# A two-layer hybrid decoder step: gated product and sum of the branches in PSUM, the residual rebuilt by pairs behind the mix, one gate chunk rounded ahead of a wait

## The chip, the cores and the metric

The kernel runs on one core of a Trainium2 chip. The metric is the time of one execution on the device, in microseconds; the median of three runs of the kernel before is 1038.56 us (1033.41 to 1039.5).

## What is computed

One inference step of a decoder with two layers, for 256 prompt tokens and 32 sample tokens (288 columns), model width 1024. Cut to what matters here:

```python
z = x @ w_in                                   # conv branch, attention branch, g_a, g_b
conv_out = silu(layer_norm(conv)) @ w_conv_out
attn_out = o @ w_attn_out                      # o: three gated attentions
mixed = sigmoid(g_a) * conv_out + sigmoid(g_b) * attn_out
x = layer_norm(ALPHA * x + mixed @ w_o, ln1_g, ln1_b)
h = silu(x @ w_gate) * (x @ w_up)
x = layer_norm(ALPHA * x + h @ w_down, ln2_g, ln2_b)
```

All is fp32. Activations are kept transposed: 128 channels on the partitions, 288 tokens in the free dimension, so `x` is 8 blocks of 128x288, and `h` is 22.

## The kernel before

**Products in three parts.** To multiply in fp32 with the `fp32r` format, each operand is split in a rounded high part and the rest, its low part. Each 128x128 block of weights costs three matmuls: high by high (L692, L730, L713), low weight by high (L693, L731, L714) and high weight by low (L694, L732, L715).

**Weights.** They come in 116 chunks per layer, of 8 blocks of 128x128 (512 KB). Each chunk goes through a ring: SyncE loads it into one of three raw buffers (`wch`), as soon as GpSimd is done with the chunk three before; ScalarE writes its high part (`high_part`, L1103, `w_hi<-wch`), as soon as TensorE is done with the chunk three before; GpSimd writes the low part (`low_part`, L620, four instructions of 128x256, `w_lo<-wch,w_hi`); TensorE then uses it. Each engine works through its program in the order in which it is written, and all waits are on semaphores written out by hand; there is no scheduler. So where a `high_part` stands among ScalarE's other instructions decides when GpSimd gets its work.

**Outputs.** Each output block of 128x288 goes to one of two PSUM banks (`proj`), in turn. TensorE starts an output when the one two before has been read (`out_read`) and its weights' low part is there (`lo_ready`).

**The stage around the change.** Per layer:

- Branch outputs: 8 blocks of `conv_out`, then 8 of `attn_out` (`branch_out`, 12 matmuls each, two blocks to a chunk). The gates stand as tanh in `gate_a` and `gate_b` (both inside the tile `hid`, which is the name in the profile). For each block VectorE runs `merge` (L1850): gate = (gate + 1) * bank. That is sigmoid times the branch, times 2.
- The mix: after each of the 8 `attn_out` blocks VectorE adds both products (L1929, `hid<-hid`), ScalarE rounds the sum to `mix_hi` (L1108), VectorE writes `mix_lo` (L1926, `low_mixed`). After every second block ScalarE also does one `high_part`.
- Ahead of the mix VectorE rebuilds the residual `x` from its high and low part in one instruction over 2304 columns (L1921, `res<-x_hi,x_lo`, signal `x_sum`), and ScalarE multiplies it by ALPHA, also in one (L1108, `res<-res`, signal `ax_ready`).
- Output projection `w_o`: 8 blocks of 24 matmuls, here WO0 to WO7. VectorE adds each to the residual (L1598, `features_in`), and from the fifth on the statistics of the layer norm are worked out.
- Feed-forward: gate and up blocks in turn, 24 matmuls each, here GU0 to GU43. For each pair ScalarE applies tanh, then rounds two chunks (`high_part`), the first of which in a layer waits behind the first normalised gate block (`gate_normed`, L1966).

The second layer runs the same program.

Of the kernel before, what the change touches and what calls it, by code (L numbers as in the profile page):

```python
# [19 lines left out]
F32 = mybir.dt.float32  # L20
F32R = mybir.dt.float32r
I32 = mybir.dt.int32
ALU = mybir.AluOpType
ACT = mybir.ActivationFunctionType
# [4 lines left out]
TOK = SEQ + DEC_B * DEC_T  # L29
# [117 lines left out]
def decoder_kernel(nc, xT, consts, page_table, weights, small, w1, w2, cmp_pages, slc_pages, win, past_u,  # L147
                   yT, kv_out, p_conv_out, s_conv_out, win_out):
    with ExitStack() as ctx:
# [124 lines left out]
        conv_mean, conv_var = ps_g[:, 0:TOK], ps_m[:, 0:TOK]  # L274
        seed_ps, mean_ps, square_ps = ps_o[:, 0:TOK], ps_s[:, 0, 0:TOK], ps_s[:, 1, 0:TOK]
        sum_ps = ps_w[:, 0:TOK]
        second_squares, third_squares = ps_t[:, :, 0:TOK], ps_s[:, :, 0:TOK]
        rstd_ps, tanh_ps, up_ps, product_ps = ps_w[:, 0:TOK], ps_o[:, 0:TOK], ps_g[:, 0:TOK], ps_s[:, 1, 0:TOK]
        SEED = KD // 2
# [72 lines left out]
        gpt_act = Signal("gpt_act", 2)  # L352
        uexp = Signal("uexp", 8)
        upt_ready = Signal("upt_ready", 8)
        ax_ready = Signal("ax_ready", 1)
        x_ready = Signal("x_ready", 2 * KD)
        ffn_tanh = Signal("ffn_tanh", KF)

# [12 lines left out]
        normed = Signal("normed", 10)  # L371
        nsa_ready = Signal("nsa_ready", 1)
        x_lo_ready = Signal("x_lo_ready", 3 * KD)
        x_sum = Signal("x_sum", 1)
        hid_lo_ready = Signal("hid_lo_ready", KF)
        gate_normed = Signal("gate_normed", KF)
        hid_ready = Signal("hid_ready", KF)
# [706 lines left out]
        def _(act):  # L1084
# [11 lines left out]
            def high_part(layer, n):  # L1096

                user, back = before(n, CHUNKS, PAIRS)
                act.wait_ge(*chunk_in[n % SLOTS](layer, n // SLOTS + 1))

                signal, count = last_use(user)
                act.wait_ge(*signal(layer, count - back * signal.per_layer))
                hi_ready.up(nc.scalar.activation(w_hi[:, n % PAIRS].rearrange("p k n -> p (k n)"),  # L1103
                                                 wch[:, n % SLOTS].rearrange("p k n -> p (k n)"), ACT.Copy))

            def do(out, in_, func, sig=None, wait=True, **kw):

                i = nc.scalar.activation(out, in_, func, **kw)  # L1108
                sig = sig or act_order
                n = sig.up(i)  # L1110
                if wait:
                    act.wait_ge(*sig(now["layer"], n))
# [154 lines left out]
            with layers(act) as layer:  # L1267
# [133 lines left out]

                for which in range(2):
                    if which == 0:
                        act.wait_ge(*x_sum(layer, 1))
                        do(res[:], res[:], ACT.Copy, ax_ready, scale=ALPHA)
                        for c in range(KD):
                            act.wait_ge(*mixed_ready(layer, c + 1))
                            do(mix_hi[:, c], gate_a[:, c], ACT.Copy, x_hi_ready, wait=False)
                            if c % 2:
                                high_part(layer, CH_IN + (KD + c) // 2 + PAIRS)  # L1410
                        for n in range(KD - 1):
                            high_part(layer, CH_IN + CH_MIX + PAIRS + n)
                            if n == 1:
                                do(warm[:], eps[:, 0:1], ACT.Sqrt, wait=False)
                            if n == SEED:
                                for pair in range(2):
                                    features_square(layer, 0, pair)
                                    features_high(layer, 2 * pair)
                                    features_high(layer, 2 * pair + 1)
                            if n >= SEED:  # L1420
                                features_square(layer, 0, n - 2)
                                features_high(layer, n)
                        features_square(layer, 0, KD - 3)
                        features_high(layer, KD - 1)
                        features_root(layer, 0)
                        high_part(layer, CH_IN + CH_MIX + PAIRS + KD - 1)
                        do(warm[:], eps[:, 0:1], ACT.Tanh, wait=False)
                    else:
                        for i in range(KF):
                            act.wait_ge(*gate_normed(layer, i + 1))  # L1430
                            do(gate_n, normed_g, ACT.Identity, bias=sums_of[:, i % 2, 1:2])
                            if i:
                                act.wait_ge(*hid_ready(layer, i))
                            do(tanh_ps, gate_n, ACT.Tanh, ffn_tanh, wait=False, scale=0.5)
                            high_part(layer, FIRST_GU + 2 * i + PAIRS)
                            high_part(layer, FIRST_GU + 2 * i + PAIRS + 1)
                            if 2 <= i < 2 + KD:
                                c = i - 2
                                act.wait_ge(*normed(layer, 3 + c // 2))
                                do(resv[:, c], resv[:, c], ACT.Identity, x_ready, scale=alpha_gb[:, c:c + 1],  # L1440
                                   bias=alpha_gb[:, KD + c:KD + c + 1], wait=False)
                            act.wait_ge(*hid_ready(layer, i + 1))
                            do(hid_hi[:, i], product_ps, ACT.Copy, hid_hi_ready, wait=False)
                        do(warm[:], eps[:, 0:1], ACT.Sqrt, wait=False)
                        n = SEED
                        for c in range(CH_DOWN - 1):
                            if n < KD - 1 and 8 * c + 7 >= KF * (n + 1) + 8:
                                if n == SEED:
                                    features_square(layer, 1, 0)
                                    features_square(layer, 1, 1)  # L1450
                                features_square(layer, 1, n - 2)
                                n += 1
                            j = CHUNKS - CH_DOWN + PAIRS + c
                            high_part(*((layer, j) if j < CHUNKS else (layer + 1, j - CHUNKS)))
                        assert n == KD - 1
                        features_square(layer, 1, n - 2)
                        features_root(layer, 1)
                        high_part(layer + 1, 2)
                        gn, bn = s("g2"), s("b2")
                        for c in range(KD):  # L1460
                            if c % 2 == 0:
                                act.wait_ge(*normed(layer, 7 + c // 2))
                            do(resv[:, c], resv[:, c], ACT.Identity, x_ready, scale=gn[:, c:c + 1], bias=bn[:, c:c + 1], wait=False)
                            if c:
                                act.wait_ge(*x_ready(layer, KD + c))
                                do(x_hi[:, c - 1, 0:TOK], resv[:, c - 1], ACT.Copy, x_hi_ready, wait=False)
                        act.wait_ge(*x_ready(layer, 2 * KD))
                        do(x_hi[:, KD - 1, 0:TOK], resv[:, KD - 1], ACT.Copy, x_hi_ready, wait=True)
                        do(warm[:], eps[:, 0:1], ACT.Tanh, wait=False)
# [7 lines left out]
        def _(dve):  # L1477
# [15 lines left out]
            def do(i, sig=None, wait=True):  # L1493
                sig = sig or dve_order
                n = sig.up(i)
                if wait:
                    dve.wait_ge(*sig(now["layer"], n))
# [85 lines left out]
            def features_in(layer, which, low):  # L1583
# [10 lines left out]

                for n in range(KD):
                    o = first + n
                    dve.wait_ge(*out_done(layer, o + 1))
                    read_out(o, v.scalar_tensor_tensor(out=resv[:, n], in0=bank[o % 2][:, 0:TOK], scalar=0.5, in1=resv[:, n],  # L1598
                                                       op0=ALU.mult, op1=ALU.add))
# [165 lines left out]
            with layers(dve) as layer:  # L1765
# [152 lines left out]
                low_attention(1, slice(3, 4))  # L1918

                dve.wait_ge(*ut_done(layer, 8))  # L1920
                do(v.tensor_tensor(resv, x_hi[:, :, 0:TOK].bitcast(F32), x_lo[:, :, 0:TOK].bitcast(F32), ALU.add), x_sum)  # L1921

                def low_mixed(c):

                    dve.wait_ge(*x_hi_ready(layer, c + 1))
                    do(v.tensor_tensor(mix_lo[:, c], gate_a[:, c], mix_hi[:, c].bitcast(F32), ALU.subtract), x_lo_ready, wait=False)  # L1926
                for n in range(KD):
                    merge(KD + n)
                    do(v.tensor_tensor(gate_a[:, n], gate_a[:, n], gate_b[:, n], ALU.add), mixed_ready, wait=False)  # L1929
                    if n:  # L1930
                        low_mixed(n - 1)
                low_mixed(KD - 1)

                def low_shifted(c):

# [18 lines left out]
                    read_out(o, v.scalar_tensor_tensor(out=out, in0=mean_sb, scalar=sums_at[:, 0:1], in1=bank[o % 2][:, 0:TOK],  # L1954
                                                       op0=ALU.mult, op1=ALU.add))

                dve.wait_ge(*ax_ready(layer, 1))
                features_in(layer, 0, low_shifted)
                take_variance(layer, 0, sd)
                for i in range(KF):  # L1960
# [123 lines left out]
```

## Time and profile before

| | |
|---|---|
| median of three runs | 1038.56 us (1033.41, 1038.56, 1039.5) |
| the profiled execution | 1034.15 us |
| its span, first to last instruction | 1032.4 us |
| mean granted clock of TensorE | 0.989 |
| TensorE matmuls busy | 979.1 us, 95% |
| GpSimd busy | 753.1 us, 73% |
| VectorE busy | 602.1 us, 58% |
| ScalarE busy | 524.2 us, 51% |

All rows below are of the profiled execution; times count from the start of its span, and 1.75 us lie around it. PE is TensorE, PEld its weight loads, DVE VectorE, ACT ScalarE, POOL GpSimd, SPq SyncE's DMA queue. In a row of the timeline the first number is the start, the second the length (of all its instructions, if x2 and more), and in brackets stands how long the engine had been idle before it and what ended that.

### The profile page before, as it was taken

Reading aid. Unit: us, or ns where it says so; the run is one execution under the profiler, and the core shown is the slowest. Engines: PE = TensorE matmul, PEld = TensorE weight load, DVE = VectorE, ACT = ScalarE, POOL = GpSimd, SP = SyncE. Lnnn points to the kernel's source line nnn. Section 1 sums busy time; section 2 is a strip of 40 time slices with the busy share of each in tenths; the row PEclk is TensorE's granted clock in tenths of the full one; section 3 lists DMA queues with packets and bytes.
Section 4 is the critical chain, followed back from the end, with each engine's and each line's share of the span. In section 5 each row is a group of like instructions: output and inputs, shape, how many; then the busy total and the mean of one; then the engine's idle time right before and its main releaser. Section 6 shows DMA issues by size and latency. Waiting matters only on the chain.

```text
span 1032.4 us, 23314 instructions
## 1 busy us (share of the span) xinstructions
PE 979.1 (95%) x7438; PEld 929.8 (90%) x7438; DVE 602.1 (58%) x1370; ACT 524.2 (51%) x966; POOL 753.1 (73%) x1081
## 2 busy tenths in 40 slices
PE   6999989999999999999999999899999999999996
PEld 6997878788989999999999978887789999999996
DVE  2969675567577555512457895844775765554125
ACT  4352674455556655533454335654545565555335
POOL 7877745434978888898867785634369788889985
PEclk9999999999999999999999999999999999999998
DMA  8985686612546755555457566684225354555543
GB/s 287 308 276 188 194 274 213 231 63 63 168 153 205 246 189 164 163 180 159 138 175 235 170 184 203 225 263 167 63 82 164 126 165 163 164 165 176 168 144 108
DMA packets 78917, 185.09 MB, mean 179 GB/s; under 512 B 9538, under 2 KB 42690, under 8 KB 78530
## 3 DMA queue, kind: packets, MB, share of 16 engines
q1 hardware_dynamic: 70288, 167.03, 50.0%
q10 hardware_dynamic: 8354, 15.59, 4.6%
q8 instruction: 62, 1.02, 0.5%
q0 software_dynamic: 144, 0.89, 0.3%
q14 instruction: 69, 0.57, 0.2%
HBM read 170.90 MB, written 12.57 MB: 178 GB/s over the span
## 4 chain that ended last, share of the span: by engine, by line
POOL 52%; issue 25%; PE 20%; POOLq 1%; DMA 1%; DVE 1%; ACT 1%; ACTq 0%; SPq 0%; DVEq 0%
POOL w_lo L620 46%; PE proj L692 4%; PE proj L694 4%; PE proj L693 4%; POOL hid L644 3%; POOL res L642 3%; PE proj L715 2%; PE proj L713 2%; PE proj L714 2%; DMA res<-xT_in 1%; POOLq L639 0%; POOLq L614 0%; POOL res L651 0%; DVE res L1575 0%; DVE sig_u L1642 0%
## 5 line engine op out<-in xcount | busy, mean ns | idle before, releaser
L620 POOL TENSOR_TENSOR w_lo<-wch,w_hi 128x256 fp32r<-128x256 f32 x940 | 685.9, 765 | 262.1 <-ACT w_hi L1103 261.8
L692 PE MATMUL proj<-x_hi,w_hi 128*128 128x290 f32 (+1 forms) x1248 | 381.9, 306 | 16.6 <-POOL w_lo L620 13.5
L694 PE MATMUL proj<-x_lo,w_hi 128*128 128x290 f32 (+1 forms) x1248 | 373.5, 299 | 0.0
L693 PE MATMUL proj<-x_hi,w_lo 128*128 128x290 f32 (+1 forms) x1248 | 372.6, 299 | 0.0
L1103 ACT ACTIVATE w_hi<-wch 128x1024 fp32r<-128x1024 f32 x235 | 247.7, 1055 | 145.2 <-PE proj L715 84.2
L692 PEld LDWEIGHTS proj<-x_hi,w_hi 128*128 128x128 f32 x1248 | 238.7, 191 | 22.2 <-DVE x_lo L1489 9.6
L693 PEld LDWEIGHTS proj<-x_hi,w_lo 128*128 128x128 f32 x1248 | 239.1, 192 | 0.6
L694 PEld LDWEIGHTS proj<-x_lo,w_hi 128*128 128x128 f32 x1248 | 238.5, 191 | 0.0
L713 PE MATMUL proj<-hid_hi,w_hi 128*128 128x288 f32 x352 | 104.4, 296 | 0.0
L715 PE MATMUL proj<-hid_lo,w_hi 128*128 128x288 f32 x352 | 104.1, 296 | 0.0
L714 PE MATMUL proj<-hid_hi,w_lo 128*128 128x288 f32 x352 | 103.5, 294 | 0.0
L1514 DVE SCALAR_TENSOR_TENSOR ps_s<-u_p,sm,ps_s 128x256 f32<-128x256 f32 x232 | 94.5, 483 | 4.2
L1598 DVE SCALAR_TENSOR_TENSOR res<-proj,res 128x288 f32<-128x288 f32 x32 | 14.6, 455 | 132.8 <-PE proj L715 111.2
L1953 DVE COPY sums_of<-proj 128x2 f32<-128x2 f32 x88 | 14.0, 159 | 99.7 <-PE proj L694 99.5
L714 PEld LDWEIGHTS proj<-hid_hi,w_lo 128*128 128x128 f32 x352 | 66.3, 188 | 0.1
L713 PEld LDWEIGHTS proj<-hid_hi,w_hi 128*128 128x128 f32 x352 | 66.1, 188 | 0.1
L715 PEld LDWEIGHTS proj<-hid_lo,w_hi 128*128 128x128 f32 x352 | 66.0, 187 | 0.0
L1108 ACT ACTIVATE q_raw<-q_raw,sums_of 128x288 f32<-128x288 f32 x44 | 23.6, 537 | 75.4 <-DVE q_raw L1966 75.4
L1108 ACT ACTIVATE res<-res,unit_top 128x128 f32<-128x128 f32 (+2 forms) x96 | 37.6, 394 | 31.8 <-DVE unit_top L1671 31.7
L692 PE MATMUL proj<-mix_hi,w_hi 128*128 128x288 f32 x128 | 38.9, 304 | 0.6 <-POOL w_lo L620 0.6
L693 PE MATMUL proj<-mix_hi,w_lo 128*128 128x288 f32 x128 | 37.8, 295 | 0.0
L694 PE MATMUL proj<-mix_lo,w_hi 128*128 128x288 f32 x128 | 37.7, 294 | 0.0
(288 smaller groups left out, 1519.7 us busy)
## 6 DMA issues: line engine op xcount, KB each, us to landing
wch<-weights_in SPq DMA_DIRECT2D x235, 512.0 KB, 3.7
pg<-slc_pages_in SPq DMA_DIRECT2D x128, 128.0 KB, 2.5
pg<-cmp_pages_in SPq DMA_DIRECT2D x96, 128.0 KB, 3.1
wn<-win_in SPq DMA_DIRECT2D x16, 512.0 KB, 5.1
win_out<-wn ACTq DMA_DIRECT2D x4, 2048.0 KB, 9.5
pg<-cmp_pages_in ACTq DMA_DIRECT2D x32, 128.0 KB, 4.5
hid<-w_in SPq DMA_DIRECT2D x2, 1024.0 KB, 6.1
kv_out<-kv ACTq DMA_DIRECT2D x2, 864.0 KB, 3.5
```

What stands on the lines that cost most here:

```text
L620: last = nc.gpsimd.tensor_tensor(lo[:, cols], raw[:, cols], hi[:, cols].bitcast(F32), ALU.subtract)
L642: do(nc.gpsimd.tensor_tensor(dst, u_s[:, :, :, tap:tap + DEC_T], tap_weight(conv_w[:, :, tap]), ALU.mult))
L644: do(nc.gpsimd.tensor_tensor(out, out, tap_s[:], ALU.add))
L692: mm(ps, hi[:, kb], x[0][:, kb, 0:n], start=kb == 0, stop=False)
L693: mm(ps, lo[:, kb], x[0][:, kb, 0:n], start=False, stop=False)
L694: last = mm(ps, hi[:, kb], x[1][:, kb, 0:n], start=False, stop=kb == KD - 1)
L713: mm(ps, hi, hid_hi[:, kb], start=kb == 0, stop=False)
L714: mm(ps, lo, hid_hi[:, kb], start=False, stop=False)
L715: last = mm(ps, hi, hid_lo[:, kb], start=False, stop=kb == KF - 1)
L1103: hi_ready.up(nc.scalar.activation(w_hi[:, n % PAIRS].rearrange("p k n -> p (k n)"), wch[:, n % SLOTS].rearrange("p k n -> p (k n)"), ACT. ...
L1108: i = nc.scalar.activation(out, in_, func, **kw)
L1514: i = v.scalar_tensor_tensor(out=out, in0=in_, scalar=conv_w[:, c, tap:tap + 1], in1=so_far, op0=ALU.mult, op1=ALU.add)
```

## The change

1. `merge` of the `attn_out` blocks no longer writes back over the gate in SBUF: the product goes to a PSUM bank (`sum_ps`, in the tile `ps_w`), and the sum with the `conv_out` product to one of four other PSUM places (`mixed_ps`, in `ps_s` and `ps_t`), in turn. ScalarE and `low_mixed` read it there.
2. The rebuild of `x` is cut in four instructions of two blocks (576 columns), and stands behind the last `low_mixed`, no longer ahead of the first merge. ScalarE's scaling by ALPHA is cut alike and stands behind the eight `mix_hi`, between the `high_part`s of `w_o`'s chunks. `features_in` waits for the pairs one by one.
3. In the feed-forward the `high_part` of chunk GU3 moves ahead of the wait for the first normalised gate block.

```diff
+        mixed_ps = [ps_s[:, 0, 0:TOK], ps_s[:, 1, 0:TOK], ps_t[:, 0, 0:TOK], ps_t[:, 1, 0:TOK]]
...
-        ax_ready = Signal("ax_ready", 1)
+        ax_ready = Signal("ax_ready", 4)
...
-        x_sum = Signal("x_sum", 1)
+        x_sum = Signal("x_sum", 4)
...
                     if which == 0:
-                        act.wait_ge(*x_sum(layer, 1))
-                        do(res[:], res[:], ACT.Copy, ax_ready, scale=ALPHA)
+                        def scale_x(n):
+                            act.wait_ge(*x_sum(layer, n + 1))
+                            do(resv[:, 2 * n:2 * n + 2], resv[:, 2 * n:2 * n + 2], ACT.Copy, ax_ready, wait=False, scale=ALPHA)
                         for c in range(KD):
                             act.wait_ge(*mixed_ready(layer, c + 1))
-                            do(mix_hi[:, c], gate_a[:, c], ACT.Copy, x_hi_ready, wait=False)
+                            do(mix_hi[:, c], mixed_ps[c % 4], ACT.Copy, x_hi_ready, wait=False)
                             if c % 2:
                                 high_part(layer, CH_IN + (KD + c) // 2 + PAIRS)
+                        scale_x(0)
                         for n in range(KD - 1):
+                            if n < 3:
+                                scale_x(n + 1)
                             high_part(layer, CH_IN + CH_MIX + PAIRS + n)
...
                     else:
+                        high_part(layer, FIRST_GU + PAIRS)
                         for i in range(KF):
                             act.wait_ge(*gate_normed(layer, i + 1))
...
-                            high_part(layer, FIRST_GU + 2 * i + PAIRS)
+                            if i:
+                                high_part(layer, FIRST_GU + 2 * i + PAIRS)
                             high_part(layer, FIRST_GU + 2 * i + PAIRS + 1)
...
                 for n in range(KD):
                     o = first + n
+                    if which == 0 and n in (0, 2, SEED):
+                        dve.wait_ge(*ax_ready(layer, n // 2 + (2 if n == SEED else 1)))
                     dve.wait_ge(*out_done(layer, o + 1))
...
                 dve.wait_ge(*ut_done(layer, 8))
-                do(v.tensor_tensor(resv, x_hi[:, :, 0:TOK].bitcast(F32), x_lo[:, :, 0:TOK].bitcast(F32), ALU.add), x_sum)
+
+                def add_x(n):
+                    blocks = slice(2 * n, 2 * n + 2)
+                    do(v.tensor_tensor(resv[:, blocks], x_hi[:, blocks, 0:TOK].bitcast(F32), x_lo[:, blocks, 0:TOK].bitcast(F32), ALU.add),
+                       x_sum, wait=False)
 
                 def low_mixed(c):
 
                     dve.wait_ge(*x_hi_ready(layer, c + 1))
-                    do(v.tensor_tensor(mix_lo[:, c], gate_a[:, c], mix_hi[:, c].bitcast(F32), ALU.subtract), x_lo_ready, wait=False)
+                    do(v.tensor_tensor(mix_lo[:, c], mixed_ps[c % 4], mix_hi[:, c].bitcast(F32), ALU.subtract), x_lo_ready, wait=False)
                 for n in range(KD):
-                    merge(KD + n)
-                    do(v.tensor_tensor(gate_a[:, n], gate_a[:, n], gate_b[:, n], ALU.add), mixed_ready, wait=False)
+                    o = O_MIX + KD + n
+                    if n:
+                        dve.wait_ge(*mixed_ready(layer, n))
+                    dve.wait_ge(*out_done(layer, o + 1))
+                    read_out(o, v.scalar_tensor_tensor(out=sum_ps, in0=gate_b[:, n], scalar=1.0, in1=bank[o % 2][:, 0:TOK],
+                                                       op0=ALU.add, op1=ALU.mult))
+                    do(v.tensor_tensor(mixed_ps[n % 4], gate_a[:, n], sum_ps, ALU.add), mixed_ready, wait=False)
                     if n:
                         low_mixed(n - 1)
                 low_mixed(KD - 1)
+                for n in range(4):
+                    add_x(n)
...
-                dve.wait_ge(*ax_ready(layer, 1))
                 features_in(layer, 0, low_shifted)
```

VectorE, from the low part of the attention output into the mix, before:

```order
L1859 TENSOR_TENSOR attn_lo<-u_p,attn_hi 128x288
L1921 TENSOR_TENSOR res<-x_hi,x_lo 128x2304
L1849 REGISTER_ALU
L1850 SCALAR_TENSOR_TENSOR hid<-hid,proj 128x288
L1502 REGISTER_ALU
L1929 TENSOR_TENSOR hid<-hid 128x288
```

and now:

```order
L1868 TENSOR_TENSOR attn_lo<-u_p,attn_hi 128x288
L1944 REGISTER_ALU
L1945 SCALAR_TENSOR_TENSOR ps_w<-hid,proj 128x288
L1509 REGISTER_ALU
L1947 TENSOR_TENSOR ps_s<-hid,ps_w 128x288
```

The 2304-column rebuild is gone from between them, and the product and the sum have PSUM tiles as their outputs.

VectorE, from the last two low parts of the mix to the reading of WO0, now (before, L1598 followed L1926 at once):

```order
L1939 TENSOR_TENSOR mix_lo<-ps_t,mix_hi 128x288
L1933 TENSOR_TENSOR res<-x_hi,x_lo 128x576 x4
L1605 ISA
L1606 REGISTER_ALU
L1607 SCALAR_TENSOR_TENSOR res<-proj,res 128x288
```

The four pieces of the rebuild stand between the mix and the first read of a bank of `w_o`.

ScalarE, from the last two `mix_hi` to the fifth chunk of `w_o` and beyond, now (before, the scalings were one instruction `res<-res` of 128x2304 ahead of the first `mix_hi`):

```order
L1109 ACTIVATE mix_hi<-ps_t 128x288 x2
L1100 REGISTER_ALU
L1103 REGISTER_ALU
L1104 ACTIVATE w_hi<-wch 128x1024
L1406 ISA
L1109 ACTIVATE res<-res 128x576
L1406 REGISTER_ALU
L1109 ACTIVATE res<-res 128x576
L1100 REGISTER_ALU
L1103 REGISTER_ALU
L1104 ACTIVATE w_hi<-wch 128x1024
```

Two scalings stand ahead of the `high_part` of WO3, one ahead of that of WO4 and one ahead of that of WO5.

ScalarE at the start of the feed-forward, before:

```order
L1103 ACTIVATE w_hi<-wch 128x1024
L1108 ACT_TABLE_LOAD
L1108 ACTIVATE warm<-eps 128x1
L1430 ISA
L1108 ACTIVATE q_raw<-q_raw,sums_of 128x288
L1112 REGISTER_ALU
L1108 ACTIVATE ps_o<-q_raw 128x288
```

and now:

```order
L1104 ACTIVATE w_hi<-wch 128x1024
L1109 ACT_TABLE_LOAD
L1109 ACTIVATE warm<-eps 128x1
L1100 REGISTER_ALU
L1103 REGISTER_ALU
L1104 ACTIVATE w_hi<-wch 128x1024
L1436 ISA
L1109 ACTIVATE q_raw<-q_raw,sums_of 128x288
```

The high part of GU3 stands ahead of the wait and of the first gate block's bias; that of GU4 follows the tanh alone.

## Rows read from the trace of the kernel before

**Rows 1.** Page, part 1: busy time and share of each engine.

```profile
PE 979.1 (95%) x7438; PEld 929.8 (90%) x7438; DVE 602.1 (58%) x1370; ACT 524.2 (51%) x966; POOL 753.1 (73%) x1081
```

**Rows 2.** Waits of PE: line, waited for, us in total, times, longest.

```profile
PE proj L692 <- POOL w_lo L620: 14.1, 7, 9.6
...
PE proj L730 <- DVE hid L1850: 2.8, 2, 1.4
...
PE proj L730 <- POOL w_lo L620: 0.8, 2, 0.4
```

**Rows 3.** Timeline of PE, first layer, from the mix to GU3.

```profile
249.82 0.29 PE L732 MATMUL proj<-attn_lo,w_hi 128*128 128x288 f32 x1
251.52 0.39 PE L730 MATMUL proj<-attn_hi,w_hi 128*128 128x288 f32 x1 [1.41 <-DVE hid L1850]
251.75 0.30 PE L731 MATMUL proj<-attn_hi,w_lo 128*128 128x288 f32 x1
...
258.56 0.40 PE L730 MATMUL proj<-attn_hi,w_hi 128*128 128x288 f32 x1 [0.42 <-POOL w_lo L620]
262.29 0.40 PE L692 MATMUL proj<-mix_hi,w_hi 128*128 128x288 f32 x1 [0.29 <-POOL w_lo L620]
303.16 0.40 PE L692 MATMUL proj<-x_hi,w_hi 128*128 128x290 f32 x1 [1.50 <-POOL w_lo L620]
```

**Rows 4.** Timeline of DVE, first layer, rebuild, mix and a sum in PSUM.

```profile
247.84 2.98 DVE L1921 TENSOR_TENSOR res<-x_hi,x_lo 128x2304 f32<-128x2304 f32 x1
...
256.00 0.99 DVE L1926 TENSOR_TENSOR mix_lo<-hid,mix_hi 128x288 fp32r<-128x288 f32 x1
256.92 0.44 DVE L1850 SCALAR_TENSOR_TENSOR hid<-hid,proj 128x288 f32<-128x288 f32 x1
257.40 0.52 DVE L1929 TENSOR_TENSOR hid<-hid 128x288 f32<-128x288 f32 x1
...
258.74 0.44 DVE L1850 SCALAR_TENSOR_TENSOR hid<-hid,proj 128x288 f32<-128x288 f32 x1
...
273.05 0.47 DVE L1603 TENSOR_TENSOR ps_w<-ps_w,res 128x288 f32<-128x288 f32 x1
```

**Rows 5.** Timeline of ACT, first layer, scaling, first and second `high_part` of the mix.

```profile
250.85 2.13 ACT L1108 ACTIVATE res<-res 128x2304 f32<-128x2304 f32 x1 [3.84 <-DVE res L1921]
253.69 1.05 ACT L1103 ACTIVATE w_hi<-wch 128x1024 fp32r<-128x1024 f32 x1
```

**Rows 6.** POOL, groups by form: 255 to 265.5 us, then 272 to 279 us.

```profile
L620 POOL TENSOR_TENSOR w_lo<-wch,w_hi 128x256 fp32r<-128x256 f32 x12 | 11.0, 951 | 6.4 <-ACT w_hi L1103 6.4
...
L620 POOL TENSOR_TENSOR w_lo<-wch,w_hi 128x256 fp32r<-128x256 f32 x11 | 7.7, 744 | 0.0
```

**Rows 7.** DVE and POOL, end of the first layer: 576 columns with two inputs in SBUF.

```profile
512.75 1.17 DVE L1575 TENSOR_TENSOR res<-res,sig_u 128x576 f32<-128x576 f32 x1
514.62 1.19 DVE L1575 TENSOR_TENSOR res<-res,sig_u 128x576 f32<-128x576 f32 x1
517.54 0.75 DVE L1575 TENSOR_TENSOR res<-res,sig_u 128x576 f32<-128x576 f32 x1
...
513.26 4.04 POOL L620 TENSOR_TENSOR w_lo<-wch,w_hi 128x256 fp32r<-128x256 f32 x4
```

**Rows 8.** ACT, then POOL, at the start of the feed-forward of the first layer.

```profile
296.53 0.20 ACT L1108 ACTIVATE warm<-eps 128x1 f32<-128x1 f32 x1
298.26 0.54 ACT L1108 ACTIVATE q_raw<-q_raw,sums_of 128x288 f32<-128x288 f32 x1 [1.53 <-DVE q_raw L1966]
299.19 1.99 ACT L1103 ACTIVATE w_hi<-wch 128x1024 fp32r<-128x1024 f32 x2
...
295.30 2.82 POOL L620 TENSOR_TENSOR w_lo<-wch,w_hi 128x256 fp32r<-128x256 f32 x4 [3.45 <-ACT w_hi L1103]
300.31 11.16 POOL L620 TENSOR_TENSOR w_lo<-wch,w_hi 128x256 fp32r<-128x256 f32 x16 [2.19 <-ACT w_hi L1103]
```

**Rows 9.** Engines' busy time from GU3 to near the feed-forward's end.

```profile
303.20:500.00 196.80, 196.80 (x1466) 196.69 (x1467) 93.72 (x214) 98.70 (x138) 173.49 (x247) 1.00 0.57 184
```

## The prediction

> **What bounds the kernel now.** I read the page's busy times first: TensorE's matmuls are busy 95% of the span, no other engine over 73% [rows 1]. The change touches no matmul, so it can only take away time in which TensorE waits. Other engines' own idle time costs nothing by itself. So the next view is what TensorE waited for [rows 2]: 14.1 us on GpSimd's low parts, 2.8 us on VectorE's merge ahead of a branch output, twice, and 0.8 us there on GpSimd, twice. Of the 14.1 us, 9.6 are one wait at the start, which the change doesn't touch.
>
> The third view is TensorE's timeline from the mix to GU3 [rows 3]. The reader is to see four holes: 1.41 us before block 10 of the branch outputs (251.52), 0.42 us before block 14 (258.56), 0.29 us before WO0 (262.29) and 1.50 us before GU3 (303.16). A hole costs more than its idle time, as matmuls overlap: from 249.82 to 251.52 is 1.70 us where 0.13 is usual (in the feed-forward 1466 matmuls fill 196.8 us [rows 9]), and the next follows after 0.23, so 1.57 + 0.10 = 1.67 us are lost, the idle time and 0.26 more. By the same surcharge the others cost 0.68, 0.55 and 1.76. Together 4.66 us a layer; the second layer has the same (the counts of 2 in [rows 2]). That is 9.3 us, the most that the change can give, but for hesitations too small for these rows.
>
> **Why the holes are there.** VectorE starts the 2304-column rebuild at 247.84 and is in it for 2.98 us [rows 4]; the merge of block 8, which frees the bank for block 10, stands behind it. ScalarE waits 3.84 us for the rebuild, scales for 2.13 us, and so gets to its next `high_part` at 253.69 only [rows 5]. GpSimd, which had been idle 6.4 us, then works without a break but slowly: 951 ns for an instruction that takes 744 later [rows 6]. That is where VectorE's L1929 and L1926 run, both with two inputs in SBUF, and L1926 itself takes 0.99 us [rows 4]. So blocks 14 and 15 and WO0 wait for late low parts.
>
> **Part 1, the rebuild out of the way.** Block 9's twelve matmuls end with the one at 249.82 [rows 3], so block 8 ends at about 248.4, and VectorE is free since 247.8: the merge is done by 248.9, and block 10 starts on time, at 249.95 (249.82 + 0.13). The first hole goes: 1.67. ScalarE can round the second sum when block 9 is merged and added (out at 250.1, two instructions of 0.48, so 251.1), and starts the `high_part` at 251.5 in place of 253.69. GpSimd starts at 252.7.
>
> **Part 2, product and sum in PSUM.** Each of the three VectorE instructions of a block then has at most one input in SBUF. Price of the PSUM form: L1603 (one PSUM input, PSUM output) takes 0.47, the merge with its PSUM input 0.44 to 0.45 [rows 4]; no row has the merge with a PSUM output. I take 0.46 for each, bounded by 0.44 from below and, from above, by the 0.52 of L1929 among GpSimd's work. GpSimd's four instructions then take 4 x 0.695 = 2.8 us a chunk (7.7 us for 11 is 0.70 each [rows 6]), not 3.65. Block 14's chunk is ready at 255.5, needed at 249.95 + 4 x 1.58 = 256.3; WO0's is ready at 258.6, needed at 259.4; WO1's at 261.7, needed at 262.6. The second and third hole go: 0.68 + 0.55. VectorE's cadence changes from 1.82 us a block (256.92 to 258.74 [rows 4]) to about 1.35, under TensorE's 1.58 (12 matmuls at 0.132).
>
> **Part 3, what the rebuild costs where it now stands.** It isn't hidden there. `low_mixed` of block 7 ends at about 261.5, and the four pieces of 576 columns follow, when GpSimd is at work (WO2's low part, from 262.1). The nearest rows are L1575, also 576 columns with two SBUF inputs: 0.75 us by itself, 1.17 and 1.19 beside GpSimd, whose four instructions then take 4.04 us [rows 7]. That is 1.24 over 2.8: two pieces at 0.52 and one 288-column instruction at 0.21 (951 less 744 [rows 6]). So both alternate, at 0.6 + 0.69 = 1.3 us a piece: the pieces start at about 261.6, 262.9, 264.1 and 265.4, and three of them fall among WO2's four: 262.1 + 2.8 + 3 x 0.52 and some waiting for a first piece = 266.7. TensorE wants WO2 at 259.4 + 2 x 3.17 = 265.8. The read of WO0's bank, queued behind the pieces, ends at 266.5, and WO2 needs that too. Either way a new hole: idle 0.9, and with the surcharge 1.2 us. Bounds: nothing, if the pieces don't meet GpSimd (0.75 each, done by 264.5); 2.2 us if each piece meets a whole instruction of it. I take 1.2, since rows 7 show just this pair.
>
> The Trainium skill (SBUF — State Buffer, Who interferes with whom) says that a VectorE instruction with two SBUF inputs and a GpSimd instruction that reads SBUF exclude each other for the whole instruction, and one with at most one SBUF input doesn't contend. The trace agrees that they exclude each other, but shows a GpSimd instruction delayed by 0.52 us beside 0.75 of VectorE's. By the rule's whole instruction the new hole would be some 0.7 us a layer larger (3 x 0.23), and the forecast 1.4 us later.
>
> ScalarE's scalings: one of 2.13 us before [rows 5], four of about 0.65 now, 0.5 us more in sum, between the high parts of WO3 to WO5. TensorE needs WO3 at 270.0, and GpSimd, done with WO2 at 266.7, has it by 269.5, ScalarE's high part being there at 265.3. WO4's slack is 0.9 us and WO5's 1.2, though its load waits for the late WO2. Cost 0; if that cover went, 0.5 us.
>
> **Part 4, GU3 ahead of the wait.** ScalarE is done with its table and the warm-up at 296.73 and sits idle 1.53 us for the first gate block [rows 8]. GU0, whose buffer GU3 takes, is long out. The `high_part` fits in: 296.8 to 297.8, and the gate at 298.26 isn't delayed. GpSimd, free at 298.12, starts GU3 then and not at 300.31 [rows 8]: done at 300.9, needed at 301.4. The fourth hole goes: 1.76. What is late next is GU5, whose high part still hangs on the gate block of the next pair, GU2, which doesn't move: it comes about when TensorE wants it, so a few tenths may come back here; I take 0. In the 196.8 us from GU3 on the matmuls have no hole at all [rows 9], so the ring can hold that pace, narrowly.
>
> **Sum.** A layer: 1.67 + 0.68 + 0.55 - 1.2 + 1.76 = 3.46 us, two layers 6.9 us. Against the profiled execution's 1034.15 us (span 1032.4 and 1.75 around it) that is 1027.2. The runs shown lie in two places, 1033.41 beside the profiled 1034.15, and 1038.56 and 1039.5; the median is in the upper, and gives 1031.6. I predict in between, 1029.5 us. A measurement of this kernel tells about 1% (10.4 us) from no change, and 6.9 is 0.7%.
>
> **Rivals.**
> - *The rebuild stays hidden.* If the pieces slip through between chunks, for VectorE gets its turn sooner than in rows 7, the whole 9.3 us come: 1024.9 by the profiled execution, 1029.3 by the median. For it: GpSimd pauses 0.4 us (261.7 to 262.1) just when the first piece starts. Against: rows 7.
> - *A hole only moves.* TensorE ahead by some 3 us finds the next link late: GU5, which comes just in time at best, or loads whose order on SyncE's queue stays tied to GpSimd. With 1 us back at GU5 and 1 us in WO3 to WO5, each layer, 2.9 us are left: 1031.2 to 1035.6. For it: slacks under 1.3 us all along part 3. Against: rows 9; in the feed-forward the links hang on TensorE's own pace.
> - *PSUM operands make VectorE the bound (slower).* Three instructions a block, all with PSUM on a side. At 0.25 us more each the cadence is 2.1 us a block, against TensorE's 1.58: the mix then ends 7 x 0.5 = 3.6 us late, and with the 1.2 for the rebuild that eats all 4.66. Slower from there on: at 0.35 us more it is 2.4, 8 x 0.3 = 2.4 us a layer further, 1039 to 1043. Against: 0.47 for L1603 and 0.44 for the merge.
>
> **Chances.** The forecast 0.50, the hidden rebuild 0.22, the moved hole 0.22, the slower case 0.06. The range: down to 1023 (the hidden rebuild, less 2 for small hesitations that go too), up to 1036 (the moved hole from the median). Faster by over 1%: half of the hidden rebuild, which lands at 0.9%, and a quarter of the forecast, as the executions scatter by 5 us: 0.24. Slower by over 1% only at the slower case's end: 0.03. Within 1%: 0.73.
>
> **What would show it.** Right: no idle time before block 10, block 14, WO0 and GU3; L620 at about 745 ns through the mix; merges 1.58 us apart; a hole of about 0.9 us before WO2, with L620 over 1200 ns three times beside the 576-column pieces. Wrong: `low_mixed` or the sum above 0.55 us; no hole before WO2 (then the first rival); holes before WO3 to WO5 or GU5, on GpSimd (the second); a granted clock off 0.989, which would change more than all of this.

## The result and the profile after

The changed kernel takes 1029.08 us (median of 8 runs, 1027.48 to 1030.35). The kernel before, run beside it and counted with its earlier three, takes 1035.47 us (8 runs, 1033.41 to 1039.5). The ratio is 0.9931, 95% interval 0.9911 to 0.9952: 6.4 us less, against a forecast of 6.9 and a predicted time of 1029.5. The profiled executions have spans of 1032.4 and 1025.7 us, 6.7 apart, with granted clocks of 0.989 and 0.991.

What TensorE waited for, after (line, waited for, us in total, times, longest), the answer to [rows 2]:

```profile
PE proj L693 <- POOL w_lo L621: 11.9, 5, 9.7
...
PE proj L731 <- DVE attn_lo L1868: 0.7, 2, 0.3
```

The wait for the merge (2.8 us) and the one of L730 for GpSimd (0.8 us) are gone from the list. Of the 11.9 us, 9.7 are the wait at the start. The timeline of PE shows in the mix, `w_o` and the feed-forward of each layer one hole only, where [rows 3] have four:

```profile
266.75 0.29 PE L694 MATMUL proj<-mix_hi,w_lo 128*128 128x288 f32 x1
266.89 0.29 PE L695 MATMUL proj<-mix_lo,w_hi 128*128 128x288 f32 x1
267.81 0.40 PE L693 MATMUL proj<-mix_hi,w_hi 128*128 128x288 f32 x1 [0.64 <-POOL w_lo L621]
268.05 0.30 PE L694 MATMUL proj<-mix_hi,w_lo 128*128 128x288 f32 x1
...
772.41 0.40 PE L693 MATMUL proj<-mix_hi,w_hi 128*128 128x288 f32 x1 [0.65 <-POOL w_lo L621]
```

That is the first matmul of WO2. From 266.89 to 267.81 are 0.92 us, 0.13 are usual, and the next follows after 0.24, so 0.79 + 0.11 = 0.90 us are lost.

VectorE, after, the answer to [rows 4]:

```profile
248.25 0.70 DVE L1868 TENSOR_TENSOR attn_lo<-u_p,attn_hi 128x288 fp32r<-128x288 f32 x1 [0.58 <-ACT attn_hi L1109]
249.71 0.46 DVE L1945 SCALAR_TENSOR_TENSOR ps_w<-hid,proj 128x288 f32<-128x288 f32 x1 [0.76 <-PE proj L733]
250.20 0.46 DVE L1947 TENSOR_TENSOR ps_s<-hid,ps_w 128x288 f32<-128x288 f32 x1
251.30 0.46 DVE L1945 SCALAR_TENSOR_TENSOR ps_w<-hid,proj 128x288 f32<-128x288 f32 x1 [0.64 <-PE proj L733]
...
257.65 0.46 DVE L1945 SCALAR_TENSOR_TENSOR ps_w<-hid,proj 128x288 f32<-128x288 f32 x1 [0.27 <-PE proj L733]
258.15 0.46 DVE L1947 TENSOR_TENSOR ps_s<-hid,ps_w 128x288 f32<-128x288 f32 x1
258.52 0.45 DVE L1939 TENSOR_TENSOR mix_lo<-ps_s,mix_hi 128x288 fp32r<-128x288 f32 x1
259.23 0.46 DVE L1945 SCALAR_TENSOR_TENSOR ps_w<-hid,proj 128x288 f32<-128x288 f32 x1 [0.27 <-PE proj L733]
...
262.63 4.54 DVE L1933 TENSOR_TENSOR res<-x_hi,x_lo 128x576 f32<-128x576 f32 x4
267.10 1.02 DVE L1607 SCALAR_TENSOR_TENSOR res<-proj,res 128x288 f32<-128x288 f32 x2
```

The low part takes 0.45 us where it took 0.99. A block takes 1.58 us (257.65 to 259.23), and VectorE now waits 0.27 us in each for TensorE. The four pieces take 4.54 us; where nothing holds them up the same columns take 2.74 (the run with one input in SBUF, below), so 1.8 are waiting.

GpSimd, groups, after: the mix (253.5 to 263 us), then WO2's chunk (263 to 267.8 us), the answer to [rows 6]:

```profile
L621 POOL TENSOR_TENSOR w_lo<-wch,w_hi 128x256 fp32r<-128x256 f32 x12 | 8.5, 743 | 4.9 <-ACT w_hi L1104 4.9
...
L621 POOL TENSOR_TENSOR w_lo<-wch,w_hi 128x256 fp32r<-128x256 f32 x5 | 5.2, 1071 | 0.3 <-ACT w_hi L1104 0.3
```

951 ns became 743 in the mix, and 1071 beside the rebuild. The last of WO2's four instructions, and VectorE's read of WO0's bank, which frees it for WO2:

```profile
266.52 1.24 POOL L621 TENSOR_TENSOR w_lo<-wch,w_hi 128x256 fp32r<-128x256 f32 x1
267.10 0.44 DVE L1607 SCALAR_TENSOR_TENSOR res<-proj,res 128x288 f32<-128x288 f32 x1
```

GpSimd ends at 267.76, the read at 267.54, and the matmul starts at 267.81. So GpSimd is the last link, but the read is only 0.2 us ahead of it (in the second layer too: 772.36 and 772.13, for 772.41).

The start of the feed-forward, ACT and then POOL, the answer to [rows 8]:

```profile
295.28 0.20 ACT L1109 ACTIVATE warm<-eps 128x1 f32<-128x1 f32 x1
295.39 1.04 ACT L1104 ACTIVATE w_hi<-wch 128x1024 fp32r<-128x1024 f32 x1
297.02 0.54 ACT L1109 ACTIVATE q_raw<-q_raw,sums_of 128x288 f32<-128x288 f32 x1 [0.59 <-DVE q_raw L1985]
...
294.05 8.43 POOL L621 TENSOR_TENSOR w_lo<-wch,w_hi 128x256 fp32r<-128x256 f32 x12 [3.44 <-ACT w_hi L1104]
```

The high part of GU3 fills 1.04 us of what was idle time, the gate block behind it still waits 0.59 us for VectorE, and GpSimd goes from GU2 to GU3 and GU4 without a break.

**A ruler for the stage.** The executions differ by several us in places that have nothing to do with the change. So I measure the stretch from the matmul of block 8 that waits 0.33 us for the attention's low part to the first matmul of `w_down`. It holds all that was changed. Before and after, first layer:

```profile
247.86 0.40 PE L730 MATMUL proj<-attn_hi,w_hi 128*128 128x288 f32 x1 [0.33 <-DVE attn_lo L1859]
...
435.58 0.29 PE L713 MATMUL proj<-hid_hi,w_hi 128*128 128x288 f32 x1
```

```profile
249.00 0.40 PE L731 MATMUL proj<-attn_hi,w_hi 128*128 128x288 f32 x1 [0.33 <-DVE attn_lo L1868]
...
432.60 0.29 PE L714 MATMUL proj<-hid_hi,w_hi 128*128 128x288 f32 x1
```

| kernel | stretch, layer 1 and 2 (us) | less than before, both layers |
|---|---|---|
| before | 187.72, 187.66 | |
| after | 183.60, 183.66 | 8.12 |

8.12 us are gained there, and some 1.4 given back elsewhere: in the first layer the stretch starts 1.14 us later (249.00 against 247.86), between the stretches 0.33 more pass, behind them as much as before. The programs are the same up to that start, and it lies anywhere from 247.60 to 251.03 us in the runs below, among kernels with the same code ahead of it. So I count this as scatter of the executions. In part it is the clock: it is granted at 1.00 through both stretches in all ten traces, and falls to 0.50, the lower of its two levels (1.2 of 2.4 GHz), twice ahead of the first. In the kernel that starts latest (251.03) it is at 0.50 from 173.5 to 180.0 us, where the changed kernel has 1.00 again from 178.4 on; TensorE has a long wait for ScalarE just there: 3.2 us up to 174.6 us, and 2.7 up to 173.6 in the changed kernel. What the rest of the scatter comes of was not tried.

### The profile page after: what moved, and what is told of

The parts are those of the page before. It is cut to its first block, busy times and chain, and to the rows that moved or that the text cites. A ratio compares the mean times of both kernels' runs of the same rounds, so it can differ in the third digit from the quotient of the medians.

```text
span 1025.7 us, 23332 instructions
## 1 busy us (share of the span) xinstructions
PE 976.8 (95%) x7438; PEld 928.7 (91%) x7438; DVE 601.6 (59%) x1376; ACT 524.8 (51%) x972; POOL 753.3 (73%) x1081
## 4 chain that ended last, share of the span: by engine, by line
POOL 53%; issue 24%; PE 20%; POOLq 1%; DMA 1%; DVE 1%; ACT 1%; ACTq 0%; SPq 0%; DVEq 0%
POOL w_lo L621 46%; PE proj L693 4%; PE proj L695 4%; PE proj L694 4%; POOL hid L645 3%; POOL res L643 3%; PE proj L716 2%; PE proj L715 2%; PE proj L714 2%; DMA res<-xT_in 1%; POOLq L640 0%; POOLq L615 0%; POOL res L652 0%; DVE res L1582 0%; DVE sig_u L1651 0%
## 6 DMA issues: line engine op xcount, KB each, us to landing
hid<-w_in SPq DMA_DIRECT2D x2, 1024.0 KB, 6.0
```

## The experiments

The ratios are to the kernel before, run beside them: 1035.82 us (median of 31 runs) for the first four, 1035.42 us (11 runs) for the last four. "Lost" is counted from start to start of the matmuls, as above. A hesitation is a matmul that starts up to 0.1 us late, too little for its row to show idle time.

### The high part of GU3 alone

The kernel before, with this:

```diff
                     else:
+                        high_part(layer, FIRST_GU + PAIRS)
                         for i in range(KF):
...
-                            high_part(layer, FIRST_GU + 2 * i + PAIRS)
+                            if i:
+                                high_part(layer, FIRST_GU + 2 * i + PAIRS)
```

> The kernel before with part 4 alone (the high part of GU3 ahead of the wait). My theory: the four holes are independent, so the hole before GU3 (1.50 us idle, 1.76 lost) goes in both layers and the three others stay: from the low part of the attention output to GU3's first matmul 53.5 us in place of 55.3, span 3.5 us shorter, no new hole at GU5. Rival (a hole only moves): half of it or more comes back as idle time before GU5 or a later gate block, and the span is under 2 us shorter.

Measured: 1032.33 us (10 runs), ratio 0.9963 (0.9949 to 0.9977). The stretch takes 186.00 and 185.89 us: 1.72 and 1.77 less. The profiled span, 1033.6 us, is longer than before's, but its stretch starts only at 251.03. PE's holes:

```profile
254.69 0.39 PE L730 MATMUL proj<-attn_hi,w_hi 128*128 128x288 f32 x1 [1.41 <-DVE hid L1852]
261.73 0.40 PE L730 MATMUL proj<-attn_hi,w_hi 128*128 128x288 f32 x1 [0.42 <-POOL w_lo L620]
265.46 0.39 PE L692 MATMUL proj<-mix_hi,w_hi 128*128 128x288 f32 x1 [0.31 <-POOL w_lo L620]
```

The three holes of the mix stand as they were, the fourth is gone, and nothing new comes at GU5 or later. The rival is out, and the 1.76 us are a term by themselves.

### The change without the high part of GU3

The changed kernel with the last edit undone.

> The changed kernel without part 4. My theory: the hole before GU3 is back with 1.50 us idle, the rest is as in the changed kernel: that stretch takes 52.9 us (51.1 in the changed kernel), the span is 3.5 us longer than the changed kernel's. Rival (TensorE being earlier, the high part of GU3 comes later relative to it): over 2 us idle there.

Measured: 1032.24 us (10 runs), ratio 0.9962 (0.9947 to 0.9977); the stretch 185.40 and 185.38 us, 1.80 and 1.72 more than the changed kernel's.

```profile
267.71 0.40 PE L693 MATMUL proj<-mix_hi,w_hi 128*128 128x288 f32 x1 [0.64 <-POOL w_lo L621]
301.81 0.40 PE L693 MATMUL proj<-x_hi,w_hi 128*128 128x290 f32 x1 [1.51 <-POOL w_lo L621]
```

The hole before GU3 is back with the idle time it had. It doesn't depend on what happens in the mix. The spans were 2.5 us apart (1028.2 and 1025.7) where I expected 3.5. The missing 1.0 lies between the two stretches, where 320.02 us pass here and 320.99 in the changed kernel, in code that is the same.

### Product and sum in PSUM alone

The kernel before, with the rebuild in one piece ahead of the mix, but:

```diff
-                            do(mix_hi[:, c], gate_a[:, c], ACT.Copy, x_hi_ready, wait=False)
+                            do(mix_hi[:, c], mixed_ps[c % 4], ACT.Copy, x_hi_ready, wait=False)
...
-                    do(v.tensor_tensor(mix_lo[:, c], gate_a[:, c], mix_hi[:, c].bitcast(F32), ALU.subtract), x_lo_ready, wait=False)
+                    do(v.tensor_tensor(mix_lo[:, c], mixed_ps[c % 4], mix_hi[:, c].bitcast(F32), ALU.subtract), x_lo_ready, wait=False)
...
-                    merge(KD + n)
-                    do(v.tensor_tensor(gate_a[:, n], gate_a[:, n], gate_b[:, n], ALU.add), mixed_ready, wait=False)
...
+                    read_out(o, v.scalar_tensor_tensor(out=sum_ps, in0=gate_b[:, n], scalar=1.0, in1=bank[o % 2][:, 0:TOK],
+                                                       op0=ALU.add, op1=ALU.mult))
+                    do(v.tensor_tensor(mixed_ps[n % 4], gate_a[:, n], sum_ps, ALU.add), mixed_ready, wait=False)
```

> The kernel before with part 2 alone: product and sum in PSUM, the rebuild in one piece ahead of the mix. My theory: the hole before block 10 stays at 1.41 us idle, since the rebuild makes it; GpSimd's instructions in the mix fall from 951 to about 745 ns, so its chunk for block 14 is ready at about 0.2 us before it is wanted and the holes before block 14 and WO0 go with the two hesitations: 1.6 us a layer, span 3 us shorter. Rival (those holes come of ScalarE's late high part, 253.69, not of the port): they stay, within 0.3 us.

Measured: 1032.95 us (10 runs), ratio 0.9973 (0.9957 to 0.9988); the stretch 186.09 and 186.12 us, 1.63 and 1.54 less than before. POOL in the mix (255 to 267 us), and PE's one hole there:

```profile
L621 POOL TENSOR_TENSOR w_lo<-wch,w_hi 128x256 fp32r<-128x256 f32 x15 | 10.6, 745 | 6.9 <-ACT w_hi L1104 6.9
```

```profile
252.96 0.40 PE L731 MATMUL proj<-attn_hi,w_hi 128*128 128x288 f32 x1 [1.42 <-DVE ps_w L1933]
302.98 0.40 PE L693 MATMUL proj<-x_hi,w_hi 128*128 128x290 f32 x1 [1.50 <-POOL w_lo L621]
```

GpSimd starts as late as before, after 6.4 us of idle time, and yet the holes before block 14 and WO0 are gone. So the late start alone doesn't make them; it takes the instructions with two inputs in SBUF, beside which GpSimd needs 951 ns in place of 745 ("the port" in what follows). The rival, that they stay, is out. For block 14 the late start counts as well: with the move alone (next) GpSimd starts 2.2 us earlier, counted from the stretch's start, and is as slow as before, and that hole is gone too. It needed both. The hole before block 10 doesn't depend on where product and sum go.

### The move alone

The kernel before, with rebuild and scaling cut and moved behind the mix as in the change; product and sum in SBUF.

```diff
-                do(v.tensor_tensor(resv, x_hi[:, :, 0:TOK].bitcast(F32), x_lo[:, :, 0:TOK].bitcast(F32), ALU.add), x_sum)
...
                 low_mixed(KD - 1)
+                for n in range(4):
+                    add_x(n)
```

> The kernel before with the rebuild and the scaling cut and moved behind the mix, product and sum still in SBUF, GU3 not moved. My theory: block 10's hole goes (1.67 us), but GpSimd still takes 3.65 us a chunk in the mix where TensorE takes 3.17, so it falls behind by 0.5 us a chunk, and the pieces cost it 1.6 us more at WO2: idle before WO0, WO1 and WO2 of together 2 to 3 us a layer, so that the move alone gives between -0.5 and +1 us a layer and the span changes by less than 2 us. Rival (the move is what gives the gain): 2.5 us a layer, span 5 us shorter.

Measured: 1036.02 us (10 runs), ratio 0.9999 (0.998 to 1.0018); the stretch 187.83 and 187.85 us, 0.11 and 0.19 more than before.

```profile
259.70 0.40 PE L693 MATMUL proj<-mix_hi,w_hi 128*128 128x288 f32 x1 [0.29 <-POOL w_lo L621]
262.68 0.40 PE L693 MATMUL proj<-mix_hi,w_hi 128*128 128x288 f32 x1 [0.33 <-DVE mix_lo L1937]
263.60 0.40 PE L693 MATMUL proj<-mix_hi,w_hi 128*128 128x288 f32 x1 [0.26 <-DVE mix_lo L1937]
268.88 0.39 PE L693 MATMUL proj<-mix_hi,w_hi 128*128 128x288 f32 x1 [1.42 <-DVE res L1605]
```

The holes before blocks 10 and 14 are gone, and as much comes back: the four here lose 0.55, 0.59, 0.52 and 1.68 us with the matmuls behind them, 3.34 in all, where the mix lost 3.30 before. Two of them I hadn't named: VectorE itself is late with `mix_lo`, at 1.82 us a block. The last is released by the read of WO0's bank behind the pieces, 1.0 us after GpSimd's low part (268.76 against 267.77). The move gains nothing while VectorE and GpSimd stand in each other's way in the mix.

### The rebuild with one input in SBUF

The changed kernel, but the pieces add what stands in a PSUM place to `x_hi`; the residual is then not `x_hi` + `x_lo`, and all that follows is computed from that.

```diff
-                    do(v.tensor_tensor(resv[:, blocks], x_hi[:, blocks, 0:TOK].bitcast(F32), x_lo[:, blocks, 0:TOK].bitcast(F32), ALU.add),
+                    do(v.tensor_tensor(resv[:, blocks], x_hi[:, blocks, 0:TOK].bitcast(F32), ps_t[:, :, 0:TOK], ALU.add),
```

> The changed kernel, but the four pieces of the rebuild take their second input from a PSUM place (what stands there in the tile ps_t) and not from x_lo in SBUF; so the residual is not the sum of high and low part. Same place, same number, same columns. My theory (the new hole before WO2 is the port that VectorE and GpSimd share): the pieces take 0.70 to 0.75 us each and are through 2.9 us after the first starts (4.54 in the changed kernel), L621 stays at 745 ns for WO2's low part in place of 1250, the hole before WO2 (0.64 us idle, 0.90 lost) is gone in both layers, the stretch from the attention's low part to the first matmul of w_down takes 182.7 us in place of 183.6. Rival (the hole is the bank of WO0, read behind the pieces, or ScalarE's scalings): the hole stays at over 0.4 us.

Measured: 1026.0 us (4 runs), ratio 0.9909 (0.9891 to 0.9927); the stretch 182.68 and 182.62 us, and PE has no hole before WO2. DVE's timeline and POOL's group from 262.9 to 267.5 us:

```profile
262.38 2.74 DVE L1933 TENSOR_TENSOR res<-x_hi,ps_t 128x576 f32<-128x576 f32 x4
265.03 0.45 DVE L1607 SCALAR_TENSOR_TENSOR res<-proj,res 128x288 f32<-128x288 f32 x1
...
L621 POOL TENSOR_TENSOR w_lo<-wch,w_hi 128x256 fp32r<-128x256 f32 x7 | 4.9, 739 | 0.3 <-ACT w_hi L1104 0.3
```

Same place, same columns, same number: 2.74 us in place of 4.54, and GpSimd at 739 ns. The hole is the port's; ScalarE's scalings, which stand where they stood, cost nothing. (This kernel can't tell GpSimd's delay from that of the bank read behind the pieces, since both go with the port. The ends in the changed kernel's trace, above, put GpSimd's last, by 0.2 us.)

### Some pieces early, the rest behind

The changed kernel with three pieces back in the mix, where GpSimd is idle:

```diff
                 for n in range(KD):
                     o = O_MIX + KD + n
+                    if n < 3:
+                        add_x(n)
...
-                for n in range(4):
-                    add_x(n)
+                add_x(3)
```

> The changed kernel with three pieces of the rebuild back in the mix, one ahead of each of the first three merges, where GpSimd is idle (249.7 to 253.7 us), and the fourth behind the mix. My theory: each delays VectorE by 0.7 us, of which the idle time there (0.76, 0.64, 0.27 us) takes most, the low parts of block 14 and WO0 come 0.5 us later than in the changed kernel but still just in time, and the hole before WO2 goes: the stretch takes 182.7 us, span 1.8 us shorter than the changed kernel's. Rival (slack too small): holes before block 14 and WO0 of 0.2 us or more each take the place of the one at WO2.

Measured: 1026.04 us (6 runs), ratio to before 0.9916 (0.9897 to 0.9936); span 1024.0 us; the stretch 182.74 and 182.72 us, 0.86 and 0.94 less than the changed kernel's, and no hole before block 14, WO0 or WO2. The pieces:

```profile
248.73 1.17 DVE L1933 TENSOR_TENSOR res<-x_hi,x_lo 128x576 f32<-128x576 f32 x1
250.68 0.75 DVE L1933 TENSOR_TENSOR res<-x_hi,x_lo 128x576 f32<-128x576 f32 x1
252.58 0.75 DVE L1933 TENSOR_TENSOR res<-x_hi,x_lo 128x576 f32<-128x576 f32 x1
262.38 0.89 DVE L1933 TENSOR_TENSOR res<-x_hi,x_lo 128x576 f32<-128x576 f32 x1
```

The first still meets the end of a GpSimd instruction (1.17), the next two meet none (0.75). The same with two early and two behind:

> As the last, with two pieces early and two behind the mix. My theory: the first late piece starts before GpSimd has WO2's high part, the second costs it 0.5 us: WO2's low part is done some 0.2 us before TensorE wants it. No hole, or one under 0.1 us; the stretch takes 182.7 to 182.9 us. Rival: hole before WO2 of 0.3 us or more.

Measured: 1026.9 us (6 runs), ratio 0.9915 (0.9898 to 0.9931), the stretch 182.78 and 182.72 us, no hole. And with all four early:

> As e6, with all four pieces early, one ahead of each of the first four merges. My theory: the fourth meets GpSimd at block 14's chunk (0.5 us) and delays the fourth merge by over 1 us, so WO0's chunk is late: holes before block 14 or WO0 of together 0.3 to 1.4 us idle, and the stretch is 183 to 184.3 us. Rival: VectorE has caught up, no hole, 182.7 us.

Measured: 1027.06 us (4 runs), ratio 0.9914 (0.9896 to 0.9932), the stretch 182.99 us in both layers. Here I was wrong: no idle time over 0.1 us appears before block 14 or WO0, only two hesitations, so 0.25 us are lost and not 0.3 to 1.4. The stretch lies at the lower end of what I gave. The fourth piece cost GpSimd's chunk 0.6 us, near the 0.5 that I had (3.45 us for four instructions, where 2.84 is usual), but the fourth merge came 0.93 us late and not over 1, and VectorE had caught up three blocks later:

```profile
255.42 0.75 DVE L1933 TENSOR_TENSOR res<-x_hi,x_lo 128x576 f32<-128x576 f32 x1
256.09 0.46 DVE L1947 SCALAR_TENSOR_TENSOR ps_w<-hid,proj 128x288 f32<-128x288 f32 x1
...
260.11 0.46 DVE L1947 SCALAR_TENSOR_TENSOR ps_w<-hid,proj 128x288 f32<-128x288 f32 x1 [0.26 <-PE proj L733]
```

(In the changed kernel the fourth merge starts 5.47 us after the stretch's first matmul, here 6.40; the idle time before the seventh, the last row, is back to 0.26.)

The ruler tells these three kernels from the changed one (1.80, 1.76 and 1.28 us less over both layers); the ratios, whose intervals overlap with the changed kernel's, don't. Of those that compute everything, three early and one behind has the shortest profiled span, 1024.0 us, and the lowest median, 1026.04, but two early and two behind is 0.04 us away by the ruler, which is nothing.

## Why the prediction was right, and what was off

- **What bounds it.** TensorE's holes were all that could be gained, and they were gained: the four are gone.
- **The four terms.** GU3: 1.76 forecast, 1.72 and 1.77 by itself. Block 14 and WO0 together: 1.23 forecast; the PSUM edit alone gives 1.63 and 1.54, because two hesitations of about 0.2 us each (with the matmul behind) went with them, at mix_lo's last block in WO0 and at WO1, which I had left out of the sum. Block 10: 1.67, gone by the move. The first hesitation, in the kernel before (0.22 and 0.24 us from start to start, where 0.13 is usual):

```profile
265.05 0.29 PE L694 MATMUL proj<-mix_lo,w_hi 128*128 128x288 f32 x1
265.27 0.40 PE L692 MATMUL proj<-mix_hi,w_hi 128*128 128x288 f32 x1
265.51 0.29 PE L693 MATMUL proj<-mix_hi,w_lo 128*128 128x288 f32 x1
```

- **Costs of the forms.** 0.46 us for the merge and the sum with PSUM outputs, as taken. Cadence 1.58 us a block, TensorE's own; the slower rival had no ground.
- **The new hole.** It came where it was forecast, at WO2, by the mechanism that was forecast: three instructions of GpSimd delayed by 0.5 us each beside the pieces (4.54 and 4.55 us for four). Only its size was off: 1.2 us taken, 0.90 measured. The step that failed is the surcharge. I had 0.9 us from 265.8, where TensorE wants WO2, to 266.7, and added what a hole costs beyond its *idle time*. But that 0.9 is already from start to start; to it only the 0.10 of the matmul behind belongs. Measured are 0.79 and 0.11.
- **The sum.** 3.46 us a layer forecast, 4.12 and 4.00 measured: 0.3 for the smaller hole, 0.4 for the hesitations. In the span 6.7 us show of the 8.12, in the medians 6.4. So the forecast of 6.9 came out closer to the measured gain than its terms earned; 1.4 us of scatter outside the stretch took away what the terms had missed. That is luck; the 95% interval of the ratio means 5.0 to 9.2 us, and holds both 6.9 and 8.12.
- **The time itself.** 1029.5 takes the kernel before to stand at 1036.4, in between the profiled 1034.15 and the median of three, 1038.56. Its eight runs have 1035.47. That this choice came within 0.4 us of the measured 1029.08 is luck too.
- **The other rivals.** The rebuild did not stay hidden (4.54 us, not 4 x 0.75), and no hole moved: neither WO3 to WO5 nor GU5 waits. The two parts of the mix do depend on each other, though, which the prediction didn't work out: over both layers PSUM alone gives 3.2 us, the move alone loses 0.3, both give 4.6 (before less the change without GU3: 2.32 and 2.28).
- **A rule on the port.** The Trainium skill (SBUF — State Buffer, Who interferes with whom) says that a VectorE instruction with two SBUF inputs contends with a GpSimd instruction that reads SBUF, and that one with at most one, outside the 2-port modes, doesn't. The traces agree: GpSimd's instruction takes 743 and 739 ns where one input is in PSUM, and 1240 to 1260 beside the pieces. Held up for the whole of a piece, each would have been delayed by 0.75 us; the mean of the five instructions in that stretch, 1071 ns, gives (1071 - 743) x 5 = 1.64 us for three pieces and a part of one, about 0.5 each. There the measurement decides.

## What to carry to other kernels

Find the holes of the engine that bounds the kernel and price each from start to start, once. An instruction of 3 us ahead of an in-order queue made a hole there and had a share in another further down. Where VectorE and GpSimd work side by side, one operand in PSUM cost nothing here (0.46 us either way) and kept them from holding each other up, and an instruction that must have two inputs in SBUF belongs where GpSimd is idle, not merely where VectorE is. Work that is moved should be tried in pieces on both sides: here two or three of four pieces fitted in gaps that the whole could not use.

## What the runs showed that I had not expected

VectorE reading and writing PSUM took 0.46 us, just what L1929 takes from SBUF to SBUF in the kernel before where GpSimd is idle (0.52 beside it). ScalarE's rounding from PSUM is a little shorter (0.41 us, where it took 0.45). With all four pieces early, VectorE made up 0.93 us of delay within three blocks, at a cost of 0.25 us to TensorE. And the start of the first stretch scatters by 3.4 us (247.60 to 251.03) over executions of the same code, which is half of what the whole change gives. The medians of ten runs show the parts only roughly (3.5 us for GU3, 2.9 for PSUM, nothing for the move); the ruler inside the trace gives 3.49, 3.17 and -0.30, and each layer by itself.
